# Last round of each stage by token halves, norm intermediates in PSUM, result rows turned by transposes

## The chip, the cores and the metric

The kernel runs on one core of one Trainium2 chip. The metric is the device time of one execution in microseconds (us). Three executions of the kernel before took 2508.81, 2510.29 and 2512.57 us; the median, 2510.29, is the time before.

## What is computed

The program is a backbone of two layers on 1024 latent tokens of width 1024, with 256 context tokens in the first layer. Everything is float32. What matters for the change is this part of the reference:

```python
def swiglu(h, w_gu, w_down):
    gt, up = jnp.split(h @ w_gu, 2, axis=-1)
    return (jax.nn.silu(gt) * up) @ w_down
...
    for l in range(DEPTH):
...
        h = h + g1 * y
        h = h + g2 * swiglu(modulate(rmsnorm(h, norm2_g[l]), sh2, sc2), ffn_w_gu[l], ffn_w_down[l])
...
    return rmsnorm(h, final_g)
```

`y` is the output of a hybrid mixer (attention beside a linear recurrence) in layer 0 and of a short gated convolution in layer 1. `rmsnorm` divides each token by the root of its mean square over the 1024 channels, so a stage can start on a token only when all 1024 channels of the stage before are there. The hidden width of the feed-forward part (FFN) is 2816, which is 11 rounds of 256.

## The kernel before, in words

The stream `h` stays in SBUF, transposed: channels on partitions as 8 tiles of 128, tokens along the free axis. The tokens are worked on as two halves of 512. A product of float32 matrices is made of three matmuls in the reduced type fp32r (`product`, L757 to L759): high part of the weights by high part of the activations, low by high, high by low. A column group (`columns`, L761) is 8 k-steps of these, 24 matmuls of 128x512.

POOL splits each weight tile of 128x1024 into its two parts (`w_hi` L591, `w_lo` L594; for the out projection L690 and L700). SP's queue loads the raw weights some tiles ahead.

The stages on the path are: out projection of the mixer; FFN0 (11 rounds); short convolution mixer (4 rounds); FFN1 (11 rounds); final norm and store. An FFN round is 8 column groups (gate and up of 2 hidden tiles, for token half 0 and then 1; a pair of groups is numbered q = 0 to 3), in which ACT makes silu, DVE the product `hid_f` and ACT and DVE its parts `hid_hi` and `hid_lo`. Then follow 16 down groups (`out_groups`, L792) of 6 matmuls, 8 for token half 0 and 8 for half 1. A short convolution round has 12 column groups and the same 16 down groups. After each down group DVE adds the bank, scaled by the gate, to `h` (`update`, L1434), and two or three banks take turns.

In the last round of a stage the norm of the next stage is woven in. I number these places:

- place 0: out projection to FFN0
- place 1: last round of FFN0 to short convolution
- place 2: last round of the short convolution to FFN1
- the end: last round of FFN1 to the stored result

For each token half, ACT squares the 8 tiles of `h` (`sq`, L1122), DVE adds the squares up in SBUF (`sumsq`: L1388 copies the first, L1391 adds 7), PE sums over partitions (`norm_sum`, L775, four one-column matmuls), ACT takes the root (L1126), DVE the reciprocal and four diagonal matrices (`diag`, L1401, L1403), PE spreads them over the partitions (`norm_spread`, L782). Then for each of 8 tiles DVE makes `scaled` in SBUF (L1410), ACT `act_hi` (L1134), and DVE `act_lo` (L1416). This order of DVE is written out by hand in `last_updates` (L1462): half 1's updates and squares are interleaved with half 0's norm. On PE the sum of half 0 stands behind the 10th down group and its spread behind the 12th; the sum of half 1 stands behind the 16th, ahead of the next stage's first column group, and its spread behind that group:

```python
                    if norm is not None and idx == 9:
                        norm_sum(norm)
                    if norm is not None and norm != N_END and idx == 11:
                        norm_spread(norm)
                if norm is not None and norm != N_END:
                    norm_sum(norm + 1)
```

At the end, `h` is multiplied by a diagonal matrix of the final gains (L1106), which turns it into token rows; DVE (L1801) and ACT (L1373) scale half a row tile each, with two row buffers, and SP stores 512 KB per row tile of 128 tokens.

Of the kernel before, what the change touches and what calls it, by code (L numbers as in the profile page):

```python
# [24 lines left out]
ALU = mybir.AluOpType  # L25
# [33 lines left out]
def backbone(nc, t):  # L59
# [18 lines left out]
    with es:  # L78
# [55 lines left out]
        std = keep("std", [P, 2, 4])  # L134
        x_std = keep("x_std", [P, 3, TT + CT])
# [32 lines left out]
        conv_t = at(84, "conv_t", [P, SEQ])  # L168
# [3 lines left out]
        gain_diag = at(60, "gain_diag", [P, FT, P])  # L172
        fin_rows = at(88, "fin_rows", [P, 2, D])
# [98 lines left out]
        s_tz, s_gdiag = sem("t_pads_zero"), sem("gain_diag_ready")  # L272
        s_fscale, s_fturn, s_store = sem("fin_scale_ready"), sem("fin_turned"), (sem("stored0"), sem("stored1"))
        s_fra, s_frd = sem("fin_row_by_act"), sem("fin_row_by_dve")
# [3 lines left out]
        def alone(eng):  # L278
# [6 lines left out]
                 + [(h, a, HALF, 4, mods, MODS + SH2) for a in (0, 1)]  # L285
                 + [(h, a, HALF, None, None, None) for a in (0, 1)])
        N_X, N_CTX, N_F0, N_S, N_F1, N_END = 0, 2, 3, 5, 7, 9
# [65 lines left out]

        def used_s(i, j):
            return (s_sg, 12 * i + (3, 4, 6, 9, 10, 12)[j]) if j < 6 else (s_out, OUT_S + 16 * i + 16)
# [9 lines left out]
        def _(sp):  # L365
# [195 lines left out]

            for tt in range(TT):
                sp.wait_ge(s_fra, tt + 1)
                sp.wait_ge(s_frd, tt + 1)
                sp.dma_start(out[0, tt * P:(tt + 1) * P, :], fin_rows[:, tt % 2, :]).then_inc(s_store[tt % 2], 16)
            for tt in range(2):
                sp.wait_ge(s_store[tt], 16 * TT // 2)
# [3 lines left out]
        def _(pool):  # L571
# [170 lines left out]
            with pool.Fori(1, FT // 2) as i:  # L742
                for j in range(8):
                    split(8 * i + (U_S + j), j % 4, j % 2, used_s(i - 1, j + 4) if j < 4 else used_s(i, j - 4))
            for j in range(6):
                split(U_F1 + j, j, j % 2, used_s(FT // 2 - 1, j + 4) if j < 4 else used_f(0, ROUNDS - 1, j))
# [6 lines left out]
        def _(pe):  # L753
# [38 lines left out]
            def out_groups(n0, group, norm=None, mod=None):  # L792
# [4 lines left out]
                for idx in range(16):  # L797
# [8 lines left out]
                    if norm is not None and norm != N_END and idx == 11:  # L806
                        norm_spread(norm)
# [1017 lines left out]
```

## Time and profile before

| what | value |
| --- | --- |
| three executions, median | 2510.29 us (2508.81 to 2512.57) |
| the profiled execution | 2510.56 us, its span 2508.4 us |
| PE busy | 2439.4 us, 97% of the span |
| DVE, POOL, ACT busy | 44%, 42%, 21% |
| share of PE in the chain that ended last | 91% |
| granted TensorE clock, mean | 0.988 of full speed |

A row of a timeline gives the start, the time from start to end, the engine, the line and the tiles, and in brackets how long the engine had been idle and what released it. Matmuls overlap: a row lasts some 390 ns, but the next one starts 227 ns later. `x8` beside four instructions means that the profiler records each of these float32 matmuls twice. The granted clock is 1.00 at 2.4 GHz and 0.50 at 1.2 GHz.

### The profile page before, as it was taken

Reading aid. Unit: us, or ns where it says so; the run is one execution under the profiler, and the core shown is the slowest. Engines: PE = TensorE matmul, PEld = TensorE weight load, DVE = VectorE, ACT = ScalarE, POOL = GpSimd, SP = SyncE. Lnnn points to the kernel's source line nnn. Section 1 sums busy time; section 2 is a strip of 40 time slices with the busy share of each in tenths; the row PEclk is TensorE's granted clock in tenths of the full one; section 3 lists DMA queues with packets and bytes.
Section 4 is the critical chain, followed back from the end, with each engine's and each line's share of the span. In section 5 each row is a group of like instructions: output and inputs, shape, how many; then the busy total and the mean of one; then the engine's idle time right before and its main releaser. Section 6 shows DMA issues by size and latency. Waiting matters only on the chain.

```text
span 2508.4 us, 29518 instructions
## 1 busy us (share of the span) xinstructions
PE 2439.4 (97%) x11190; PEld 1994.9 (80%) x11190; DVE 1114.9 (44%) x1433; ACT 528.9 (21%) x811; POOL 1057.6 (42%) x507
## 2 busy tenths in 40 slices
PE   7999999989899999999999899998899999999999
PEld 3788878878788888888887788886788888888887
DVE  5566648856644443422224534346522222222224
ACT  4544428851200000000002200002200000000003
POOL 3233347888533334444443243442543333333340
PEclk9999999999999999999999999999899999999999
DMA  9444465533333333211111011111211111111111
GB/s 302 148 137 150 149 177 95 103 110 101 118 109 100 102 117 117 84 51 50 42 49 43 26 49 44 54 46 34 62 48 47 46 46 46 49 43 50 50 34 68
DMA packets 223197, 206.54 MB, mean 82 GB/s; under 512 B 40119, under 2 KB 193427, under 8 KB 222611
## 3 DMA queue, kind: packets, MB, share of 16 engines
q1 hardware_dynamic: 216643, 186.64, 25.1%
q10 hardware_dynamic: 5904, 16.78, 1.9%
q0 software_dynamic: 576, 2.10, 0.2%
q8 instruction: 51, 0.84, 0.1%
q14 instruction: 23, 0.19, 0.0%
HBM read 185.20 MB, written 20.28 MB: 82 GB/s over the span
## 4 chain that ended last, share of the span: by engine, by line
PE 91%; DVE 4%; issue 2%; ACT 2%; POOL 0%; DMA 0%; ACTq 0%; DVEq 0%; POOLq 0%; SPq 0%
PE bank L757 28%; PE bank L759 28%; PE bank L758 28%; PE bank L893 1%; PE bank L818 1%; DVE probs L1679 1%; PE bank L949 1%; DVE sumsq L1391 1%; PE bank L975 1%; PE bank L974 1%; PE bank L936 1%; PE bank L789 1%; ACT probs L1275 1%; PE bank L937 1%; DVE h L1434 1%
## 5 line engine op out<-in xcount | busy, mean ns | idle before, releaser
L591 POOL TENSOR_TENSOR w_hi<-raw,ones 128x1024 fp32r<-128x1024 f32 x184 | 361.2, 1963 | 1220.0 <-PE bank L759 1164.1
L757 PE MATMUL bank<-act_hi,w_hi 128*128 128x512 f32 x2160 | 846.1, 392 | 3.3 <-DVE act_lo L1555 2.7
L758 PE MATMUL bank<-act_hi,w_lo 128*128 128x512 f32 x2168 | 847.0, 391 | 0.0
L759 PE MATMUL bank<-act_lo,w_hi 128*128 128x512 f32 x2160 | 843.1, 390 | 0.0
L757 PEld LDWEIGHTS bank<-act_hi,w_hi 128*128 128x128 f32 x2160 | 407.5, 189 | 89.7 <-issue 2.8
L758 PEld LDWEIGHTS bank<-act_hi,w_lo 128*128 128x128 f32 x2168 | 409.6, 189 | 84.4
L759 PEld LDWEIGHTS bank<-act_lo,w_hi 128*128 128x128 f32 x2160 | 407.2, 189 | 85.3
L594 POOL TENSOR_TENSOR w_lo<-raw,w_hi 128x1024 fp32r<-128x1024 f32 x184 | 468.0, 2543 | 14.4
L1434 DVE SCALAR_TENSOR_TENSOR h<-bank,mods,h 128x512 f32<-128x512 f32 x432 | 319.7, 748 | 217.2 <-PE bank L759 216.1
L1719 DVE TENSOR_TENSOR hid_f<-silu_g,bank 128x512 f32<-128x512 f32 x88 | 60.5, 688 | 711.2 <-PE bank L759 709.9
L757 PE MATMUL bank<-hid_hi,w_hi 128*128 128x512 f32 x704 | 276.8, 393 | 3.4 <-DVE h L1434 3.2
L759 PE MATMUL bank<-hid_lo,w_hi 128*128 128x512 f32 x704 | 275.1, 391 | 0.0
L758 PE MATMUL bank<-hid_hi,w_lo 128*128 128x512 f32 x704 | 274.5, 390 | 0.0
L757 PEld LDWEIGHTS bank<-hid_hi,w_hi 128*128 128x128 f32 x704 | 132.5, 188 | 34.0 <-DVE h L1434 7.1
L759 PEld LDWEIGHTS bank<-hid_lo,w_hi 128*128 128x128 f32 x704 | 132.4, 188 | 28.5
L758 PEld LDWEIGHTS bank<-hid_hi,w_lo 128*128 128x128 f32 x704 | 132.6, 188 | 27.3
L1338 ACT CAST hid_hi<-hid_f 128x512 fp32r<-128x512 f32 x88 | 54.9, 623 | 449.2 <-DVE hid_f L1719 449.2
L1336 ACT ACT_TABLE_LOAD x20 | 25.7, 1283 | 479.0 <-PE bank L759 478.9
L1336 ACT ACTIVATE silu_g<-bank 128x512 f32<-128x512 f32 x88 | 52.8, 600 | 315.0 <-PE bank L759 314.8
L1722 DVE TENSOR_TENSOR hid_lo<-hid_f,hid_hi 128x512 fp32r<-128x512 f32 x88 | 78.5, 892 | 60.7 <-ACT hid_hi L1338 60.7
L1761 DVE TENSOR_TENSOR t_pad<-cg_sb,bank 128x512 f32<-128x512 f32 x16 | 11.0, 690 | 141.3 <-PE bank L759 141.0
L1275 ACT ACTIVATE probs<-probs,low_all 128x768 f32<-128x768 f32 (+1 forms) x64 | 63.6, 994 | 27.2 <-DVE low_all L1679 26.6
(210 smaller groups left out, 2387.1 us busy)
## 6 DMA issues: line engine op xcount, KB each, us to landing
raw<-in_ffn_w_gu SPq DMA_DIRECT2D x88, 512.0 KB, 3.9
mod_in_f<-in_mod_w SPq DMA_DIRECT2D x48, 512.0 KB, 4.6
raw<-in_ffn_w_down SPq DMA_DIRECT2D x44, 512.0 KB, 3.6
mod_in_p<-in_mod_w SPq DMA_DIRECT2D x32, 512.0 KB, 6.8
raw<-in_o_w_in SPq DMA_DIRECT2D x24, 512.0 KB, 3.7
raw<-in_e_w_in SPq DMA_DIRECT2D x20, 512.0 KB, 5.2
mod_ring<-in_mod_w SPq DMA_DIRECT2D x16, 512.0 KB, 9.5
raw<-in_e_w_out SPq DMA_DIRECT2D x16, 512.0 KB, 3.6
```

The lines of the kernel that those rows point to most:

```text
L591: nc.gpsimd.tensor_tensor(w_hi, raw[:, parity, :], ones[:, 0:1].to_broadcast([P, UNIT]), ALU.mult).then_inc(s_hi, 1)
L594: nc.gpsimd.tensor_tensor(w_lo, raw[:, parity, :], w_hi, ALU.subtract).then_inc(s_split, 1)
L757: pe.matmul(dst, w_hi, x_hi, start=first, stop=False)
L758: pe.matmul(dst, w_lo, x_hi, start=False, stop=False)
L759: return pe.matmul(dst, w_hi, x_lo, start=False, stop=last)
L789: mm = pe.matmul(bank[:, 7, m:m + 1], acc[:, m * P:(m + 1) * P], ones[:, 0:1], start=True, stop=True)
L1275: nc.scalar.activation(probs[s % 3][:, 0:w], probs[s % 3][:, 0:w], ACT.Exp, bias=low_all[:, s:s + 1], scale=-1.0, accum_out=sums[:, s:s + ...
L1336: nc.scalar.activation(silu_g[:, q % 2, :], bank[:, 2 * tile, :], ACT.Silu).then_inc(s_silu, 1)
L1338: nc.scalar.copy(hid_hi[:, tile, half * HALF:(half + 1) * HALF], hid_f[:, q % 2, :]).then_inc(s_hidh, 1)
L1434: V.scalar_tensor_tensor(out=dst, in0=bank[:, from_, :], scalar=mods[:, gate, m:m + 1], in1=dst, op0=ALU.mult, op1=ALU.add).then_inc(s_hup, 1)
L1719: V.tensor_tensor(hid_f[:, q % 2, :], silu_g[:, q % 2, :], bank[:, 2 * tile + 1, :], ALU.mult).then_inc(s_hidf, 1)
L1722: V.tensor_tensor(hid_lo[:, tile, sl], hid_f[:, q % 2, :], hid_hi[:, tile, sl], ALU.subtract).then_inc(s_hid, 1)
```

## The change

The diff runs to some 900 lines. In words:

1. In the last round of FFN0, of the short convolution and of FFN1, all column groups but those of the last tile of half 1 (FFN: q = 3) run first. Then the 8 down groups of half 0, then the groups left out, then the 8 down groups of half 1. The norm of half 0 is done beside q = 3 and the down groups of half 1 (`last_ffn_round`, `last_norms`).
2. The sum over partitions moves into a column group: it stands behind 4 of the 8 k-steps of the group that follows (`first_norm`), and the spread behind that group. This holds for both halves, and for place 0 too, where nothing else of the order changes.
3. `scaled` is written to two PSUM banks (`SCALED`), and the running sum of squares to PSUM bank 7; the last add writes `sumsq` in SBUF, which PE reads. `hid_f` and `z_f` of the part left for later are in a bank too.
4. The first round of the short convolution is ordered so that groups of half 0 come first; the convolution has two buffers.
5. At the end, PE transposes `h` (64 transposes) in place of the products with the diagonal gains. Row tiles 0 to 3 are turned inside q = 3 and the last down groups, and 5 of the 8 parts of row tiles 4 and 5 before the last down group. ACT squares a row tile with its accumulator and takes the root, DVE takes the reciprocal and multiplies 128x1024 by it and by a row of gains. There are four row buffers.

```diff
+        SCALED = {3: 2, 4: 4, 5: 0, 6: 4, 7: 2, 8: 4}
...
             def scale(n, f):
                 src, half, w, gain, *_ = NORMS[n]
                 dve.wait_ge(s_bc, n + 1)
-                dve.wait_ge(s_norm, 8 * n + f - 2)
-                V.scalar_tensor_tensor(out=scaled[:, (8 * n + f) % 3, 0:w], in0=src[:, f, cols(n)], scalar=gains[:, gain, f:f + 1],
+                dve.wait_ge(s_norm, 8 * n + f - 1)
+                V.scalar_tensor_tensor(out=bank[:, SCALED[n] + f % 2, 0:w], in0=src[:, f, cols(n)], scalar=gains[:, gain, f:f + 1],
                                        in1=bank[:, SPREAD[n], 0:w], op0=ALU.mult, op1=ALU.mult).then_inc(s_scal, 1)
...
-                    V.tensor_tensor(sumsq[:, 0:w], sumsq[:, 0:w], sq[:, f % 2, 0:w], ALU.add).then_inc(s_sum, 1)
+                    if f == FT - 1 and n > N_F0:
+                        dve.wait_ge(s_ss, n - N_F0)
+                    to = sumsq[:, 0:w] if f == FT - 1 else bank[:, 7, 0:w]
+                    V.tensor_tensor(to, bank[:, 7, 0:w], sq[:, f % 2, 0:w], ALU.add).then_inc(s_sum, 1)
```

New functions of PE (`gate_up` is one pair of groups, `half_down` 8 down groups; the fourth argument of `last_ffn_round` is None for FFN1):

```python
            def first_norm(n):
                return ({4: lambda: norm_sum(n)}, None), lambda: norm_spread(n)
...
                for q in range(3):
                    gate_up(layer, i, u0, norm_in, q)
                half_down(0, (2, 3))
                pe.wait_ge(s_hup, n0 + 6)
                if norm_out is not None:
                    gate_up(layer, i, u0, norm_in, 3, *first_norm(norm_out))
                    half_down(1, ())
                else:
                    gate_up(layer, i, u0, norm_in, 3, ({3: lambda: fin_early(0)}, {2: lambda: fin_early(1), 6: lambda: fin_early(2)}))
                    half_down(1, (), {4: lambda: fin_early(3), 6: lambda: fin_late((4, 5), range(4)), 7: lambda: fin_late((4, 5), (4,))})
```

New on DVE (`mid` holds the product of q = 3, at the third tile), and the row at the end:

```python
                def between(f):
                    if f in mid:
                        mid[f]()
                    if 3 <= f < 7:
                        for m in (2 * f - 6, 2 * f - 5):
                            update(n0, FT + m, gate, 4 + m % 2)

                apply_norm(n, between)
                for f in range(FT):
                    add_squares(n + 1, f)
                inverse_rms(n + 1)
                apply_norm(n + 1)
...
                V.reciprocal(fin_scale[:, tt:tt + 1], fin_rms[:, tt:tt + 1]).then_inc(s_fscale, 1)
...
                V.scalar_tensor_tensor(out=fin_rows[tt % 4][:], in0=bank_f[:, b * HALF:(b + 2) * HALF], scalar=fin_scale[:, tt:tt + 1],
                                       in1=gain_row[:], op0=ALU.mult, op1=ALU.mult).then_inc(s_fin, 1)
```

The order on DVE at place 1, while the norm of half 0 is applied. Before, each tile of the norm goes with an update and an add of half 1's squares:

```order
L1410 SCALAR_TENSOR_TENSOR scaled<-h,gains,bank 128x512 x2
L1416 SCALAR_TENSOR_TENSOR act_lo<-scaled,mods,act_hi 128x512
L1410 SCALAR_TENSOR_TENSOR scaled<-h,gains,bank 128x512
L1434 SCALAR_TENSOR_TENSOR h<-bank,mods,h 128x512
L1391 TENSOR_TENSOR sumsq<-sumsq,sq 128x512
L1416 SCALAR_TENSOR_TENSOR act_lo<-scaled,mods,act_hi 128x512
```

Now:

```order
L1630 SCALAR_TENSOR_TENSOR bank<-h,gains,bank 128x512
L1968 TENSOR_TENSOR bank<-silu_g,bank 128x512
L1971 TENSOR_TENSOR hid_lo<-bank,hid_hi 128x512
L1636 SCALAR_TENSOR_TENSOR act_lo<-bank,mods,act_hi 128x512
L1630 SCALAR_TENSOR_TENSOR bank<-h,gains,bank 128x512
L1653 SCALAR_TENSOR_TENSOR h<-bank,mods,h 128x512 x2
L1636 SCALAR_TENSOR_TENSOR act_lo<-bank,mods,act_hi 128x512
```

and behind the last tile of that norm:

```order
L1636 SCALAR_TENSOR_TENSOR act_lo<-bank,mods,act_hi 128x512
L1608 COPY bank<-sq 128x512
L1614 TENSOR_TENSOR bank<-bank,sq 128x512 x6
L1614 TENSOR_TENSOR sumsq<-bank,sq 128x512
L1621 RECIPROCAL std<-std 128x4
```

The product of q = 3 moved in, the updates come in pairs, and all eight squares of half 1 are added up behind the norm of half 0.

The order on PE at place 1, from the last down group into the short convolution. Before:

```order
L759 MATMUL bank<-hid_lo,w_hi 128x512
L775 MATMUL bank<-ones,sumsq 128x1 x4
L757 MATMUL bank<-act_hi,w_hi 128x512
L758 MATMUL bank<-act_hi,w_lo 128x512
L759 MATMUL bank<-act_lo,w_hi 128x512
```

Now the sum stands behind 12 matmuls of the first group, of which the last three are:

```order
L788 MATMUL bank<-act_hi,w_hi 128x512
L789 MATMUL bank<-act_hi,w_lo 128x512
L790 MATMUL bank<-act_lo,w_hi 128x512
L808 MATMUL bank<-ones,sumsq 128x1 x4
L788 MATMUL bank<-act_hi,w_hi 128x512
```

The sum moved 12 matmuls back; those need only half 0, whose norm is done.

The order on PE at the very end (`ident` is the identity, `h` the stream; L878 is the transpose). It is now:

```order
L790 MATMUL bank<-hid_lo,w_hi 128x512
L878 MATMUL bank<-ident,h 128x128 x2
L788 MATMUL bank<-hid_hi,w_hi 128x512
L789 MATMUL bank<-hid_hi,w_lo 128x512
L790 MATMUL bank<-hid_lo,w_hi 128x512
L788 MATMUL bank<-hid_hi,w_hi 128x512
L789 MATMUL bank<-hid_hi,w_lo 128x512
L790 MATMUL bank<-hid_lo,w_hi 128x512
L878 MATMUL bank<-ident,h 128x128 x22
```

22 of the 64 transposes stand behind the last down group; the other 42 moved ahead of it.

## Rows read from the trace of the kernel before

**Rows 1.** Window over the four up and gate stretches of a round: busy us, clock, DMA.
```profile
1309.25:1352.78 43.53, 43.53 (x193) 36.05 (x192) 5.31 (x7) 4.28 (x7) 21.73 (x10) 1.00 0.17 49
```

**Rows 2.** Timeline of PE, place 0: start, us, instruction, idle before in brackets.
```profile
597.08 0.95 PE L775 MATMUL bank<-ones,sumsq 128*128 128x1 f32 x8
...
639.79 1.86 PE L775 MATMUL bank<-ones,sumsq 128*128 128x1 f32 x8 [7.69 <-DVE sumsq L1391]
...
688.08 0.39 PE L757 MATMUL bank<-hid_hi,w_hi 128*128 128x512 f32 x1
```

**Rows 3.** Timeline of PE, place 1, FFN0 to short convolution.
```profile
1352.78 0.39 PE L757 MATMUL bank<-hid_hi,w_hi 128*128 128x512 f32 x1
...
1375.72 0.50 PE L757 MATMUL bank<-hid_hi,w_hi 128*128 128x512 f32 x1 [2.31 <-DVE h L1434]
...
1388.56 1.87 PE L775 MATMUL bank<-ones,sumsq 128*128 128x1 f32 x8 [6.03 <-DVE sumsq L1391]
1390.29 0.77 PE L757 MATMUL bank<-act_hi,w_hi 128*128 128x512 f32 x1
...
1397.26 1.05 PE L782 MATMUL bank<-diag,ones 128*128 128x128 f32 x8
1398.07 0.48 PE L757 MATMUL bank<-act_hi,w_hi 128*128 128x512 f32 x1
...
1459.28 0.40 PE L757 MATMUL bank<-z_hi,w_hi 128*128 128x512 f32 x1
```

**Rows 4.** Timeline of PE, place 2, short convolution to FFN1.
```profile
1721.24 0.40 PE L757 MATMUL bank<-z_hi,w_hi 128*128 128x512 f32 x1
...
1763.81 1.86 PE L775 MATMUL bank<-ones,sumsq 128*128 128x1 f32 x8 [12.73 <-DVE sumsq L1391]
...
1811.59 0.39 PE L757 MATMUL bank<-hid_hi,w_hi 128*128 128x512 f32 x1
```

**Rows 5.** Timelines of DVE and of POOL, place 2.
```profile
1749.86 0.76 DVE L1416 SCALAR_TENSOR_TENSOR act_lo<-scaled,mods,act_hi 128x512 fp32r<-128x512 f32 x1
...
1753.59 2.82 DVE L1416 SCALAR_TENSOR_TENSOR act_lo<-scaled,mods,act_hi 128x512 fp32r<-128x512 f32 x1
1756.34 0.73 DVE L1410 SCALAR_TENSOR_TENSOR scaled<-h,gains,bank 128x512 f32<-128x512 f32 x1
1756.99 0.74 DVE L1434 SCALAR_TENSOR_TENSOR h<-bank,mods,h 128x512 f32<-128x512 f32 x1
...
1768.93 2.80 DVE L1403 TENSOR_SCALAR diag<-ident,std 128x128 f32<-128x128 f32 x4
...
1753.20 2.67 POOL L594 TENSOR_TENSOR w_lo<-raw,w_hi 128x1024 fp32r<-128x1024 f32 x1
```

**Rows 6.** Windows of 2 us at place 1; the number behind the busy times is the granted clock.
```profile
1376.00:1378.00 2.00, 2.00 (x6) 1.19 (x5) 2.00 (x4) 0.94 (x2) 0.00 (x0) 0.56 0.00 0
1390.00:1392.00 2.00, 2.00 (x7) 1.71 (x7) 1.05 (x5) 0.27 (x1) 0.00 (x0) 0.50 0.00 0
```

**Rows 7.** Timeline of DVE, place 2, where POOL runs nothing.
```profile
1738.98 0.42 DVE L1388 COPY sumsq<-sq 128x512 f32<-128x512 f32 x1
1739.50 0.69 DVE L1391 TENSOR_TENSOR sumsq<-sumsq,sq 128x512 f32<-128x512 f32 x1
```

**Rows 8.** Timelines at the end: the last down matmul and the last half row.
```profile
2488.09 0.39 PE L759 MATMUL bank<-hid_lo,w_hi 128*128 128x512 f32 x1
...
2504.51 0.75 DVE L1801 TENSOR_SCALAR fin_rows<-bank,fin_scale 128x512 f32<-128x512 f32 x1 [0.75 <-DMA out<-fin_rows]
```

**Rows 9.** Timeline of PE in the attention stage, and the window around it.
```profile
442.26 0.82 PE L949 MATMUL bank<-ident,probs 128*128 128x128 f32 x6
442.84 0.48 PE L974 MATMUL bank<-pt_hi,v_odd 128*128 128x512 f32 x1
...
442.00:444.00 2.00, 2.00 (x14) 1.79 (x13) 1.41 (x4) 1.75 (x4) 1.92 (x2) 1.00 1.05 257
```

**Rows 10.** Group of ACT by line and shape: busy us, mean ns, idle before by releaser.
```profile
L1122 ACT ACTIVATE sq<-h 128x512 f32<-128x512 f32 x64 | 40.0, 632 | 93.6 <-DVE h L1434 92.1 <-DVE sumsq L1388 1.4
```

More of the change, by code:

```diff
@@ L1014, in _, with gate_up @@
             out_groups(0, out_group, N_F0)
-            def ffn_round(layer, i, u0, norm_in, norm_out=None, mod=None, first=False):
+            def gate_up(layer, i, u0, norm_in, q, at_k=None, then=None):
+                q0 = 4 * ROUNDS * layer
+                half, tile = divmod(q, 2)
+                pe.wait_ge(s_hidf, 4 * i + (q0 + q + 1))
+                for a in range(2):
+                    if half == 0:
+                        pe.wait_ge(s_split, 6 * i + (u0 + 2 * tile + a + 1))
+                    columns(bank[:, 2 * tile + a, :], 2 * tile + a, act_hi, act_lo,
+                            slice(half * HALF, (half + 1) * HALF), norm_in + half,
+                            at_k[a] if at_k is not None else None).then_inc(s_gu, 1)
+                    if then is not None and a == 0:
+                        then()
@@ new lines, in short_tile @@
+            def short_tile(i, tile, banks=(0, 2), halves=range(2)):
+                for half in range(2):
+                    cg_copy(i, tile, half, banks[half])
+                for half in halves:
+                    z_high(i, tile, half)
+            short_tile(0, 0, (2, 1))
+            short_tile(0, 1, (1, 0))
+            with act.Fori(1, SHORT_LAST) as i:
+                for tile in range(2):
+                    short_tile(i, tile)
+            short_tile(SHORT_LAST, 0, (0, 2), (0,))
@@ new lines, in short_tile @@
+            def short_tile(i, tile, banks=(1, 3), gates_=(0, 1)):
+                for half in range(2):
+                    short_half(i, tile, half, banks)
+                short_conv(i, tile)
+                for half, b in enumerate(gates_):
+                    short_z(i, tile, half, b)
+            short_tile(0, 0, (3, 2), (0, 3))
+            short_tile(0, 1, (2, 3), (1, 2))
+            for idx in range(16):
+                update(OUT_S, idx, MODS + G1, 4 + idx % 3)
+            with dve.Fori(1, SHORT_LAST) as i:
+                steps.begin_loop(i - 1, 6)
+                for tile in range(2):
+                    short_tile(i, tile)
+                for idx in range(16):
+                    update(16 * i + OUT_S, idx, MODS + G1, 4 + idx % 3)
```

537 lines of the change are left out of this document (351 added, 186 removed).

## The prediction

> **What bounds the kernel now.** I read first the chain of waits: it is TensorE's matmuls for 91% of the span, so only what stops TensorE costs time. Then a window over one stretch of column groups: 192 matmuls in 43.53 us at a granted clock of 1.00, which is 0.2267 us each, with PE busy all the time [rows 1]. Nothing can be won there. Then the timeline of PE for its idle brackets. They stand at the places where a norm lies between two stages. I take each place from its first to its last row, and subtract 0.2267 us for each matmul and 0.81 us for each of the four small blocks (two sums, two spreads); 0.81 is the step from 1397.26 to 1398.07 [rows 3].
>
> - Place 0: 688.08 - 597.08 = 91.00; 336 matmuls are 76.17, blocks 3.24; **11.6 us too much**, 7.69 of it the wait ahead of half 1's sum [rows 2].
> - Place 1: 106.50; 384 matmuls are 87.05, blocks 3.24; **16.2 us too much**: waits of 2.31 and 6.03 and what follows them [rows 3].
> - Place 2: 90.35; 288 matmuls are 65.29, blocks 3.24; **21.8 us too much**, the sum's wait alone 12.73 [rows 4].
> - The end: from the last down matmul at 2488.09 to 2508.40 it takes **20.3 us** [rows 8].
>
> What DVE does in the waits shows two causes. It has a long list between the two norms. And an operation with both tensors in SBUF is slowed while POOL splits weights: act_lo takes 0.76 us alone and 2.82 with POOL's w_lo beside it, while scaled and h, which read a bank, keep 0.73 and 0.74 at the same time [rows 5]. A third cost follows: after a wait TensorE runs slower. At place 1 the granted clock is 0.56 after the first wait and 0.50 after the second [rows 6], that is near the lower level of 1.2 GHz. Behind the second wait the sum took 1.73 us (not 0.81) and the first 24 matmuls 6.97 (not 5.44) [rows 3]: **2.45 us per such wait**.
>
> **Prices.** A DVE operation with one bank operand starts 0.65 us after the one before (1756.34 to 1756.99, rows 5); I use 0.66. No row shows one with a bank both read and written, which scaled, the copy and the adds now are. The surcharge of one bank operand can be bounded: the add of two SBUF tiles lasts 0.69, an update 0.74 [rows 5, 7]. So from 0 to 0.12 us more than now (an estimate: twice that difference). I take 0.73 for each of the eight square operations, since each waits for the one before (0.69 and a handover), and 0.66 for the rest. A rule speaks against the copy: it took 0.42 from SBUF to SBUF [rows 7]. The Trainium skill, "VectorE: DVE Perf Modes", section "Why PSUM operands drop a tier", says that a PSUM operand keeps fp32 out of the faster modes; no run here shows it yet. By the row the copy would stay at 0.42 and each place be 0.3 us shorter; by the rule it is as I have it.
>
> **Place 0.** The order on DVE stays, only tiles move to PSUM, and the sum moves behind 12 matmuls. DVE now has some 25 operations of 0.66 to 0.73, 17.5 us, ahead of the sum, from 610 on: done long before the last down matmul at 631.72 (639.79 less 7.69 less 0.39). What is late next is the last update's chain: 0.39 + 0.10 to the bank, update 0.74, square 0.63 [rows 10], add 0.69, with handovers: ready at 634.4. TensorE gets there at 631.72 + 0.23 + 12 x 0.2267 = 634.67. No wait, and no fall of the clock. The diagonals stay in SBUF and may still take 2.80 [rows 5] where 2.72 of matmuls and the block cover them: 0.7 left. Of the 11.6, some 0.9 belongs to neither wait nor clock, and I leave as much again for DVE's lag: 2.5 stay, **9.1 gained**.
>
> **Place 1.** Between half 0's spread and half 1's sum, DVE does 16 norm operations and 8 updates (24 x 0.66 = 15.84), 8 on squares (8 x 0.73 = 5.84), and for q = 3 hid_f, a cast by ACT and hid_lo (2.1, as DVE waits for ACT): 23.8. I add 2.1 for waits for ACT's first square, its halves and its reloads of tables (an estimate): 25.9. TensorE has in that time the second group (24), 48 down matmuls and 12 of the next group, 84 x 0.2267 = 19.04. So **6.9 us of wait stay**, and with them 2.45 for the clock. The hidden parts are late for the first down group of half 1, and updates for its banks: 0.95. Together 10.3 of 16.2: **5.9 gained**. POOL runs nothing there, so this is the order alone.
>
> **Place 2.** Two tiles' z for half 1 take the place of one hidden tile: 2.1 more, 28.0; less 19.04 leaves 9.0. Then 2.45 for the clock; a wait of 2.0 for the z of half 1, by the length of ACT's and DVE's steps on it, with a fall of the clock that costs 2.1 (the wait of 2.31 at place 1 had one, rows 3, 6); small ones 1.0. Together 16.5 of 21.8: **5.3 gained**. That POOL no longer slows act_lo is in this, since all of DVE's list now has at most one SBUF input but the diagonals.
>
> **The end.** Ahead of the last matmul come 42 transposes. Six took 0.58 (442.26 to 442.84, rows 9), 0.10 each; a row of a float32 block gives 0.81/4 = 0.20 each. I take 0.125, 5.25 together (bounds 4.1 and 8.5). The hidden parts of q = 3 are late by 1.0, turns of banks 0.5, while the sum and its block fall away (0.8): the last matmul is **6.0 later**. Behind it: matmul and handover 0.49, update 0.74, the last transposes 0.45, then ACT's squares and roots row tile by row tile: 1.1 each for 4 and 5, 2.2 each for 6 and 7 (two squares of 0.63 [rows 10] and small operations), DVE's last 128x1024 with its reciprocal 1.5 (two times 0.66 and a little), the store as now, 2508.40 - 2505.26 = 3.14 [rows 8], and 0.6 of handovers: 13.5. **20.3 - 13.5 = 6.8 won, 6.0 lost: 0.8 gained.** The reordered first round of the short convolution I cost at nothing: TensorE has no wait there, and DVE's work is hidden behind 24 matmuls per group; without that cover it would be a few tenths.
>
> **Sum.** 9.1 + 5.9 + 5.3 + 0.8 = 21.1. From the profiled execution, 2510.56: 2489.5. The median is 0.27 lower: **2489.2 us**.
>
> **Rivals.**
> - *A, DVE stays the bound by more.* Bank to bank costs 0.12 more in 16 operations (1.9) and the waits for ACT are 4 instead of 2: at places 1 and 2 3.9 us more each, at place 0 a short wait comes back with its clock, 4. Together 11.8: **2501**. For it: DVE's list is longer than TensorE's cover at places 1 and 2 in my own count. Against: ACT was never late there before.
> - *B, slower: the clock at the end.* 42 transposes stand among the last 96 matmuls. If TensorE's clock fell to its lower level over q = 3 and the last down groups, 96 x 0.2267 + 5.3 = 27 us would become 54: 2489.2 + 27 = **2516**. It decides against the change from 21 us at half clock on. Against it: with six transposes in two microseconds the attention stage has a granted clock of 1.00 [rows 9], and TensorE is never idle beside these. The Trainium skill, "TensorE: Matmul & The Clock Gate", Part 4 ("PE-mode transpose"), says that a transpose "doesn't count as PE-busy the same way"; by that rule the clock would be at risk, and the attention row does not bear it out.
> - *C, the tiles in PSUM do not do what they should.* If POOL slowed DVE whatever its operands, the order alone would help: place 0 keeps 7.69 less the 2.72 of the 12 matmuls and its clock, so gains some 3, place 2 about 1, places 1 and the end as above: 10.7, **2499.6**. Against it: scaled and h beside act_lo [rows 5]. The Trainium skill, "SBUF — State Buffer", section "Who interferes with whom", has it that only a second SBUF input contends, which would exclude C; the trace agrees for operations that read a bank, none shows one that also writes it.
> - *D, no change*: transposes at 0.20 (3.2 more), A and a longer tail: 2506 to 2510.
>
> **Chances.** Forecast 0.66, A 0.18, C 0.07, D 0.04, B 0.04, and 0.01 for the rest. The range goes down to **2480**, where the clock does not fall at places 1 and 2 (7.0) and bank operands cost nothing more and 2 more are won from waits; it goes up to **2501**, taking in A and C. Forecast's own range is 2482 to 2496. No difference that a measurement can tell is within 0.2%, 5 us: faster means below 2505.3. From the cases: forecast, A (but its upper end) and C make 0.91 faster; D 0.04 within; B and the rest 0.05 slower.
>
> **What would show it.** Right: PE's wait for sumsq under 1 us at place 0, with the granted clock at 1.00; 4 to 9 us of such waits at places 1 and 2, followed by a clock near 0.50; scaled, act_lo and adds below 0.8 us beside POOL; the last matmul near 2473 in the trace, and 13 to 14 us behind it. Wrong: waits for sumsq gone at places 1 and 2 (I overcounted DVE); act_lo above 2 us (C); a granted clock under 0.9 after 2440 (B).

## The result and the profile after

The changed kernel takes 2494.11 us in the median (2492.61 to 2495.64), the kernel before 2510.28. The ratio is 0.9935 with a 95% interval of 0.9922 to 0.9947: **16.2 us or 0.65% faster**. The forecast was 2489.2, range 2480 to 2501. Sign and range held; the gain was three quarters of the 21.1 us of the sum, and its parts were off in both directions.

The page of the changed kernel, busy times, granted clock and chain:

```profile
PE 2427.5 (97%) x11110; PEld 1983.5 (80%) x11110; DVE 1078.7 (43%) x1415; ACT 529.3 (21%) x825; POOL 1053.0 (42%) x507
...
PEclk9999999999999999999999999999999999999999
...
PE 92%; DVE 4%; ACT 2%; issue 1%; POOL 0%; ACTq 0%; DVEq 0%; POOLq 0%
```

PE is busy 12 us less than before (2439.4), with the same large matmuls and fewer small ones; the other 6 us of the gain are idle time. To see where, I cut the timeline of PE into the same stretches in both kernels. Place 1 runs here from the first matmul of FFN0's last round, place 2 from that of the last short convolution round, each up to the first down matmul of the next round; the end from the last FFN1 round's first matmul.

| stretch, us | before | after | gained | forecast |
| --- | --- | --- | --- | --- |
| start to the first sum of place 0 | 597.08 | 595.03 | 2.05 | 0 |
| place 0 | 91.00 | 86.19 | 4.8 | 9.1 |
| place 1 | 150.03 | 146.60 | 3.4 | 5.9 |
| short convolution, rounds 0 to 2 | 196.63 | 197.80 | -1.2 | 0 |
| place 2 | 155.68 | 149.95 | 5.7 | 5.3 |
| the end | 87.05 | 84.13 | 2.9 | 0.8 |
| all FFN rounds between | 1230.97 | 1231.10 | -0.1 | 0 |

The 2.05 us ahead of place 0 are no work of the change: in the profiles of the fourteen kernels of this study, whose first part is the same, the first sum starts anywhere from 593.83 to 597.08 us. Without it the profiled runs differ by 15.6 us, which fits the medians.

**Place 0.** PE's timeline in the changed kernel, and behind it DVE's, POOL's and two windows. A window gives its start, end and length, then the busy us and the number of instructions of PE, PE's weight loads, DVE, ACT and POOL, then the granted clock, the share of the DMA engines and GB/s:

```profile
633.18 1.05 PE L808 MATMUL bank<-ones,sumsq 128*128 128x1 f32 x8 [0.83 <-DVE sumsq L1614]
...
640.52 2.08 PE L815 MATMUL bank<-diag,ones 128*128 128x128 f32 x8 [3.43 <-DVE diag L1623]
642.25 0.77 PE L788 MATMUL bank<-act_hi,w_hi 128*128 128x512 f32 x1
...
630.94 0.74 DVE L1636 SCALAR_TENSOR_TENSOR act_lo<-bank,mods,act_hi 128x512 fp32r<-128x512 f32 x1
...
634.79 5.68 DVE L1623 TENSOR_SCALAR diag<-ident,std 128x128 f32<-128x128 f32 x4
...
634.07 1.90 POOL L618 TENSOR_TENSOR w_hi<-raw,ones 128x1024 fp32r<-128x1024 f32 x1
...
638.00:640.00 2.00, 0.00 (x0) 0.00 (x0) 2.00 (x2) 0.00 (x0) 2.00 (x2) 1.00 0.03 9
642.00:644.00 2.00, 2.00 (x7) 1.69 (x7) 1.36 (x2) 0.58 (x1) 0.85 (x1) 0.52 1.01 360
```

The sum's wait went from 7.69 us [rows 2] to 0.83, and act_lo takes 0.74 us beside POOL (2.82 before, rows 5). But now the spread waits 3.43 us for the diagonals. These four 128x128 operations, 0.88 us alone and 2.80 in [rows 5], took 5.68 us, and the clock fell behind the wait to 0.52. One by one they took 1.26, 0.28, 2.44 and 1.93 us: three of them ended within 0.1 us of the end of a POOL operation. A wait took the place of the one removed.

**Places 1 and 2.** The waits of PE, and DVE's list at place 1:

```profile
1362.74 0.50 PE L788 MATMUL bank<-hid_hi,w_hi 128*128 128x512 f32 x1 [1.36 <-DVE hid_lo L1971]
...
1381.69 1.87 PE L808 MATMUL bank<-ones,sumsq 128*128 128x1 f32 x8 [4.95 <-DVE sumsq L1614]
...
1732.31 0.50 PE L788 MATMUL bank<-z_hi,w_hi 128*128 128x512 f32 x1 [3.14 <-DVE z_lo L2031]
...
1752.03 1.86 PE L808 MATMUL bank<-ones,sumsq 128*128 128x1 f32 x8 [4.95 <-DVE sumsq L1614]
...
1357.63 0.75 DVE L1636 SCALAR_TENSOR_TENSOR act_lo<-bank,mods,act_hi 128x512 fp32r<-128x512 f32 x1
1358.48 0.76 DVE L1630 SCALAR_TENSOR_TENSOR bank<-h,gains,bank 128x512 f32<-128x512 f32 x1
...
1376.13 4.72 DVE L1614 TENSOR_TENSOR bank<-bank,sq 128x512 f32<-128x512 f32 x6
1380.94 0.69 DVE L1614 TENSOR_TENSOR sumsq<-bank,sq 128x512 f32<-128x512 f32 x1
...
1376.92 0.63 ACT L1279 ACTIVATE sq<-h 128x512 f32<-128x512 f32 x1 [0.17 <-DVE bank L1614]
...
1384.00:1386.00 2.00, 2.00 (x6) 1.61 (x5) 0.94 (x5) 0.00 (x0) 0.00 (x0) 0.50 0.00 0
```

Both sums are 4.95 us late, where they were 6.03 and 12.73 [rows 3, 4]. The clock still falls behind them: 0.50, and the 12 matmuls behind the sum at place 1 take 4.97 us in place of 2.72. From an act_lo to the next scaled DVE now steps 0.85 us, not 0.66. The six adds take 4.72 us, 0.79 each: each waits for ACT's square, and that for a buffer of an add. At place 2, PE also waits 3.14 us for the z of half 1.

The 3.4 us that place 1 gained can be split by counting what PE spends over 0.2267 us a matmul. The 96 down matmuls cost 6.4 us over before and 4.1 now, 2.3 gained; the sum's wait gave 0.9. The matmuls between the sum and the spread, slowed by the clock in both, cost 0.7 more. Behind the last spread 1.36 us over became 0.11, which is 1.25 gained by the reordered first short convolution round: before, three matmuls were held up there by act_lo of half 1 (the longest recorded wait is 0.36).

**The end.** The last down matmul, the last row, and a window in which PE transposes between matmuls:

```profile
2478.20 0.39 PE L790 MATMUL bank<-hid_lo,w_hi 128*128 128x512 f32 x1
...
2486.41 1.28 DVE L1740 SCALAR_TENSOR_TENSOR fin_rows<-bank,fin_scale,gain_row 128x1024 f32<-128x1024 f32 x1
...
2450.00:2460.00 10.00, 10.00 (x53) 8.41 (x52) 2.20 (x3) 5.48 (x7) 0.00 (x0) 1.00 0.13 53
```

From the last matmul to 2490.80 it takes 12.60 us (20.3 before, rows 8), and the stretch ahead of that matmul is 4.83 us longer. The granted clock is 1.00 with 16 transposes among the matmuls of that window.

### The profile page after: what moved, and what is told of

It reads as the page before. It is cut to its first block, busy times and chain, and to the rows that moved or that the text cites. A ratio compares the mean times of both kernels' runs of the same rounds, so it can differ in the third digit from the quotient of the medians.

```text
span 2490.8 us, 29258 instructions
## 1 busy us (share of the span) xinstructions
PE 2427.5 (97%) x11110; PEld 1983.5 (80%) x11110; DVE 1078.7 (43%) x1415; ACT 529.3 (21%) x825; POOL 1053.0 (42%) x507
## 3 DMA queue, kind: packets, MB, share of 16 engines
HBM read 185.73 MB, written 20.28 MB: 83 GB/s over the span
## 4 chain that ended last, share of the span: by engine, by line
PE 92%; DVE 4%; ACT 2%; issue 1%; POOL 0%; ACTq 0%; DVEq 0%; POOLq 0%
PE bank L788 28%; PE bank L790 28%; PE bank L789 28%; PE bank L976 1%; PE bank L901 1%; DVE probs L1928 1%; PE bank L1032 1%; PE bank L1058 1%; PE bank L1057 1%; PE bank L1019 1%; PE bank L822 1%; ACT probs L1477 1%; PE bank L1020 1%; DVE bank L1614 0%; DVE h L1653 0%
```

## The experiments

Edits are shown in part; `...` marks what is left out. before_psum, before_sum_inside, before_both and tiles_sbuf take the change apart, with two theories. **Theory 1**, mine: where POOL runs, DVE is slowed in operations with both tensors in SBUF; the rest is DVE's list against TensorE's cover. **Theory 2**: the order is what counts. Where theory 2 says something else, the expectation tells. All stretches are taken as above, each from the one profiled execution of its kernel. The time before is the median of all its executions beside these runs (2510.2 to 2510.4 each time).

| kernel | median | place 0 | place 1 | short | place 2 | the end |
| --- | --- | --- | --- | --- | --- | --- |
| before | 2510.4 | 91.0 | 150.0 | 196.6 | 155.7 | 87.0 |
| changed | 2494.1 | 86.2 | 146.6 | 197.8 | 150.0 | 84.1 |
| before_psum | 2504.5 | 86.8 | 153.6 | 196.6 | 151.3 | 87.3 |
| before_sum_inside | 2506.2 | 89.8 | 148.3 | 196.6 | 157.3 | 87.1 |
| before_both | 2500.2 | 87.3 | 150.3 | 196.6 | 149.9 | 87.3 |
| before_two_buffers | 2514.4 | 91.0 | 153.4 | 196.6 | 157.6 | 87.0 |
| tiles_sbuf | 2506.9 | 91.6 | 150.8 | 197.8 | 154.2 | 84.2 |
| end_late | 2502.4 | 86.1 | 146.6 | 197.8 | 150.0 | 93.1 |
| end_late_banks | 2498.1 | 86.2 | 147.2 | 197.8 | 150.5 | 87.0 |
| diag_act | 2488.8 | 80.9 | 146.5 | 197.8 | 151.5 | 84.2 |
| sum_later | 2489.8 | 87.0 | 144.1 | 197.8 | 148.0 | 84.1 |
| squares_early | 2474.4 | 81.2 | 138.8 | 197.8 | 144.0 | 84.2 |
| z_early | 2474.6 | 81.2 | 138.9 | 197.8 | 143.0 | 84.2 |
| scale_last | 2474.1 | 81.8 | 138.8 | 197.8 | 142.2 | 84.2 |

A stretch moves by up to 1.5 us with how long the clock stays down behind the same waits: diag_act has at place 2 the waits of the changed kernel (3.16 and 4.95 us, there 3.14 and 4.95) and takes 1.5 us more, all of it in the matmuls behind the second wait and in the spread. Differences of about a microsecond between two rows of a place are not told apart by this table.

### before_psum: the tiles in PSUM alone

```diff
-                dve.wait_ge(s_norm, 8 * n + f - 2)
+                dve.wait_ge(s_norm, 8 * n + f - 1)
...
-                V.scalar_tensor_tensor(out=scaled[:, (8 * n + f) % 3, 0:w], in0=src[:, f, cols(n)], scalar=gains[:, gain, f:f + 1],
+                V.scalar_tensor_tensor(out=bank[:, SCALED[n] + f % 2, 0:w], in0=src[:, f, cols(n)], scalar=gains[:, gain, f:f + 1],
...
-                    V.tensor_tensor(sumsq[:, 0:w], sumsq[:, 0:w], sq[:, f % 2, 0:w], ALU.add).then_inc(s_sum, 1)
+                    to = sumsq[:, 0:w] if f == FT - 1 else bank[:, 7, 0:w]
+                    V.tensor_tensor(to, bank[:, 7, 0:w], sq[:, f % 2, 0:w], ALU.add).then_inc(s_sum, 1)
```

> The kernel before, with scaled and the running sum of squares in PSUM; its order untouched. Theory 1 (beside POOL, DVE is slowed where both tensors of an operation lie in SBUF): act_lo and the adds stay at 0.7 to 0.8 us beside POOL; the sum's wait falls from 7.69 to about 2.5 us at place 0 and from 12.73 to about 6 at place 2, place 1 stays within 0.5 us; the diagonals, still in SBUF, take over 2.8 us at place 0. Time 12 to 14 us under the kernel before, about 2497. Theory 2 (the order is what counts): the waits stay within 2 us of before, time 2507 to 2510.

Measured: ratio 0.9972 (0.9960 to 0.9983). DVE at place 0, and PE's waits at places 0 and 2:

```profile
632.38 0.74 DVE L1418 SCALAR_TENSOR_TENSOR act_lo<-bank,mods,act_hi 128x512 fp32r<-128x512 f32 x1
...
636.86 4.99 DVE L1405 TENSOR_SCALAR diag<-ident,std 128x128 f32<-128x128 f32 x4
...
634.63 1.68 PE L776 MATMUL bank<-ones,sumsq 128*128 128x1 f32 x8 [3.55 <-DVE sumsq L1393]
...
1756.98 1.86 PE L776 MATMUL bank<-ones,sumsq 128*128 128x1 f32 x8 [5.56 <-DVE sumsq L1393]
```

act_lo is fast beside POOL, and the waits fell about as theory 1 had it (3.55 us at place 0 where it said 2.5, 5.56 at place 2 where it said 6; the diagonals took 4.99). With the kernel's order untouched, this shows both the contention and its cure. But place 1, where both theories saw nothing, lost 3.6 us, and the total was 7 us short of what theory 1 gave.

### before_two_buffers: why place 1 lost

```diff
-                dve.wait_ge(s_norm, 8 * n + f - 2)
-                V.scalar_tensor_tensor(out=scaled[:, (8 * n + f) % 3, 0:w], in0=src[:, f, cols(n)], scalar=gains[:, gain, f:f + 1],
+                dve.wait_ge(s_norm, 8 * n + f - 1)
+                V.scalar_tensor_tensor(out=scaled[:, f % 2, 0:w], in0=src[:, f, cols(n)], scalar=gains[:, gain, f:f + 1],
```

> The kernel before, with two buffers for scaled in SBUF in place of three, so that each scaled waits for the act_lo just ahead of it. Theory 1 (the pair of PSUM banks costs 0.19 us a tile through this wait, not through PSUM): DVE's step from act_lo to the next scaled grows from 0.66 to 0.85 us at place 1, and place 1 takes 2.5 to 4 us more, as it did with the tiles in PSUM (153.6 in place of 150.0). Theory 2 (writing PSUM is what is dear): place 1 stays within 0.5 us of 150.0.

Measured: ratio 1.0015 (1.0005 to 1.0024), place 1 at 153.4, beside 153.6 with the tiles in PSUM. DVE at place 1:

```profile
1377.84 0.75 DVE L1416 SCALAR_TENSOR_TENSOR act_lo<-scaled,mods,act_hi 128x512 fp32r<-128x512 f32 x1
1378.69 0.75 DVE L1410 SCALAR_TENSOR_TENSOR scaled<-h,gains,bank 128x512 f32<-128x512 f32 x1
```

The step is 0.85 us, in SBUF as in PSUM. Theory 1 holds: a bank costs DVE nothing that shows (0.74 to 0.76 us for each of these operations). What costs is a turn of two: scaled of tile f + 2 must wait for the end of act_lo of tile f, just ahead of it on the same engine. That is 0.19 us for each of six tiles, 1.1 us, ahead of the sum and again behind its spread; the remaining 1.0 of the 3.3 us lost is the clock, behind a sum's wait of 6.60 in place of 6.03.

### before_sum_inside: the sum inside a group alone

```diff
                 for k in range(FT):
+                    if k == 4 and at_k is not None:
+                        norm_sum(at_k)
...
-                if norm is not None and norm != N_END:
-                    norm_sum(norm + 1)
```

> The kernel before, with the sum of half 1 moved behind 12 matmuls of the next stage's first group, the spread still behind that group; all tiles stay in SBUF. Theory 1: the sum's waits fall by 2.7 us at each place, but at places 0 and 2 the diagonals (2.8 us, behind two act_lo of 5.1 us, both slowed by POOL) are then late for the spread, and a wait of some 3.5 us ahead of it takes the gain back; only place 1 gains, 2.7 us, or 5 if the clock does not fall. Time 2505 to 2508. Theory 2: 2.7 us and the clock's 2.45 at each place, 2495 to 2500.

Measured: ratio 0.9980 (0.9971 to 0.9990). At place 2, DVE and the wait behind it:

```profile
1756.37 5.13 DVE L1418 SCALAR_TENSOR_TENSOR act_lo<-scaled,mods,act_hi 128x512 fp32r<-128x512 f32 x2
1761.42 0.16 DVE L1403 RECIPROCAL std<-std 128x4 f32<-128x4 f32 x1
1761.62 6.52 DVE L1405 TENSOR_SCALAR diag<-ident,std 128x128 f32<-128x128 f32 x4
...
1768.20 2.08 PE L784 MATMUL bank<-diag,ones 128*128 128x128 f32 x8 [5.24 <-DVE diag L1405]
```

The time is theory 1's, its parts only in kind. The sum's waits fell by 2.72 and 2.74 us at places 0 and 1 (7.69 to 4.97, 6.03 to 3.29), as said. At place 2 it fell by 7.31 (12.73 to 5.42), in part since one act_lo and one add fewer met POOL's splits ahead of the sum; and there the spread then waited 5.24 us behind two act_lo in 5.13 and four diagonals in 6.52. At place 0 it waited 1.01, not 3.5. Place 1 gained 1.7 where 2.7 was expected, place 0 1.2, and place 2 lost 1.7. The sum's step by itself is worth little.

### before_both: the two together

> Both edits together on the kernel before: tiles in PSUM and the sum inside the first group; no halves order, and the old end. Theory 1: place 0 as in the changed kernel (about 5 us gained), place 1 some 3 to 5 gained, place 2 some 9 to 11 gained: about 2491 to 2493, so the order by halves of the last round adds nothing at places 1 and 2. Theory 2 (the order by halves brings its own gain there): 2 to 5 us more than the changed kernel at places 1 and 2 together, 2498 to 2503.

Measured: ratio 0.9957 (0.9940 to 0.9974), 10.2 us under before. The time fits theory 2, the places show why. Place 0 is as in the changed kernel but for 1.1 us, with nearly the same wait for the diagonals (3.34); the 1.1 us are slower matmuls behind the spread (2.0 us over 0.2267 each, 0.9 in the changed kernel), so the clock. Place 2 gained 5.8, as much as the changed kernel and not the 9 to 11 I expected. Place 1 gained nothing (150.3), as the turn of two ate what the sum won. So **the order by halves and the reordered first short round are worth 3.7 us at place 1 and nothing at place 2**, and the changed kernel gives 1.2 of it back in the short convolution rounds. By PE's timeline the 3.7 are 2.6 in the down groups and 2.35 behind the spread, the part of the short round, less 1.1 of a longer wait for the sum. No run has the one without the other.

### tiles_sbuf: the changed kernel without scaled in PSUM

```diff
-                V.scalar_tensor_tensor(out=bank[:, SCALED[n] + f % 2, 0:w], in0=src[:, f, cols(n)], scalar=gains[:, gain, f:f + 1],
+                V.scalar_tensor_tensor(out=scaled[:, f % 2, 0:w], in0=src[:, f, cols(n)], scalar=gains[:, gain, f:f + 1],
```

> The changed kernel, with scaled back in SBUF (two buffers), all else as changed; the sums stay in PSUM. Theory 1: act_lo takes 2.5 to 2.9 us where POOL runs: place 0 loses 4 to 6 us, place 1 some 2 to 3 (POOL splits four tiles there beside the norm of half 0), place 2 some 6 to 8: about 2508. Theory 2 (where the tile lies does not matter in this order): within 2 us of the changed kernel, 2492 to 2496.

Measured: ratio to before 0.9986 (0.9977 to 0.9996), 12.8 us over the changed kernel: place 0 lost 5.4, places 1 and 2 4.2 each. DVE at place 0, one act_lo and then the last two with the diagonals:

```profile
632.09 1.28 DVE L1636 SCALAR_TENSOR_TENSOR act_lo<-scaled,mods,act_hi 128x512 fp32r<-128x512 f32 x1
...
634.74 3.69 DVE L1636 SCALAR_TENSOR_TENSOR act_lo<-scaled,mods,act_hi 128x512 fp32r<-128x512 f32 x2
...
638.56 6.53 DVE L1623 TENSOR_SCALAR diag<-ident,std 128x128 f32<-128x128 f32 x4
```

Theory 1 holds, with the total at 2506.9 for 2508; of its parts place 1 lost more than the 2 to 3 us said and place 2 less than the 6 to 8. Where scaled lies carries most of the gain of the changed kernel: four fifths of 16.2 us go with it. That is against two buffers in SBUF; with three, as the kernel before has, it may be less, and I did not run that. In this order the spread at place 0 waits 5.68 us.

### diag_act: the diagonals by ACT

```diff
+                for j in range(NORMS[n][2] // P):
+                    last = nc.scalar.activation(diag[:, j, :], ident[:], ACT.Copy, scale=std[:, 1, j:j + 1])
+                last.then_inc(s_rstd, 1)
...
-                for j in range(w):
-                    last = V.tensor_scalar(diag[:, j, :], ident[:], std[:, 1, j:j + 1], None, ALU.mult)
-                last.then_inc(s_rstd, 1)
```

> The changed kernel, with the four diagonal matrices of each norm written by ACT (a copy scaled per partition) in place of DVE. Theory 1 (at place 0 the gain is held back by the diagonals alone, two SBUF tensors on DVE beside POOL, 5.68 us): ACT takes about 1.0 us for the four, the 3.43 us wait ahead of the spread and the clock's fall behind it go, place 0 falls from 86.2 to about 81 us, the other places stay within 0.3; 5 us under the changed kernel, 2489. Theory 2 (place 0 is held by something else, such as act_hi's latency or the loads, and the diagonals only stand last): place 0 keeps over 84 us, 2492 to 2494.

Measured: 2488.79 us (2488.60 to 2490.87), ratio to before 0.9914 (0.9897 to 0.9930), 5.3 under the changed kernel. ACT and PE at place 0:

```profile
636.75 1.28 ACT L1288 ACTIVATE diag<-ident,std 128x128 f32<-128x128 f32 x4 [0.24 <-DVE std L1626]
...
638.90 1.05 PE L816 MATMUL bank<-diag,ones 128*128 128x128 f32 x8
```

The four take 1.28 us beside POOL's split, the spread has no wait, and place 0 falls from 86.2 to 80.9: theory 1, to 0.1 us. Everything I missed at place 0 was in the diagonals; the wait of 0.83 us at the sum is still there. Place 2 was to stay within 0.3 us and took 1.5 more in this profile. Its waits did not change, the clock behind them did: in the last 2 us ahead of the spread it is 0.50 here and 0.82 in the changed kernel (second row).

```profile
1753.64:1755.64 2.00, 2.00 (x6) 1.52 (x5) 0.00 (x0) 0.00 (x0) 0.00 (x0) 0.50 0.00 0
...
1755.92:1757.92 2.00, 2.00 (x8) 1.57 (x8) 0.00 (x0) 0.00 (x0) 0.00 (x0) 0.82 0.29 86
```

### sum_later: more cover ahead of the sum

```diff
-                short_group(0, 0, 0, 0, 2, (s_hid, 4 * ROUNDS), sums[0])
-                spread()
-                short_group(0, 0, 1, 0, 3, (s_zf, 2))
+                short_group(0, 0, 0, 0, 2, (s_hid, 4 * ROUNDS))
+                norm_sum(N_S + 1)
+                short_group(0, 0, 1, 0, 3, (s_zf, 2), {4: lambda: norm_spread(N_S + 1)})
```

> The changed kernel, with the sum of half 1 behind the whole first group of the next stage (24 matmuls in place of 12) and the spread behind 12 matmuls of the second group, at all three places. Theory 1 (places 1 and 2 are short of cover for DVE's list): the waits of 4.95 fall to 2.2 and the clock stays up, each place gains 2.7 for the wait and 2.5 for the clock; place 0 gains 0.8: 2483 to 2486. Theory 2 (the late norm then holds the groups of half 1 or the banks that hid_f must free): the wait moves there, gain 0 to 3 us, 2491 to 2494.

Measured: 2489.83 us (2489.23 to 2491.05), ratio 0.9920 (0.9903 to 0.9936). PE at place 1 and the clock behind its wait:

```profile
1382.92 1.87 PE L808 MATMUL bank<-ones,sumsq 128*128 128x1 f32 x8 [2.23 <-DVE sumsq L1613]
...
1384.00:1386.00 2.00, 2.00 (x7) 1.79 (x8) 0.84 (x5) 0.26 (x1) 0.00 (x0) 0.50 0.00 0
```

The wait fell to 2.23 us as said, and place 1 gained 2.5, place 2 2.0, so the wait's part came. The clock's part did not: behind 2.23 us the granted clock is again 0.50. At place 2, whose wait was 2.23 us too, it fell again. Place 0 lost 0.8: its wait only moved to the diagonals (3.92). Both theories had part of it wrong: the waits did not move to other groups, and the clock did not stay up.

### squares_early: both, and three adds moved up

```diff
-                        for m in (2 * f - 6, 2 * f - 5):
-                            update(n0, FT + m, gate, 4 + m % 2)
+                        update(n0, FT + 2 * f - 6, gate, 4)
+                        if f in (4, 6):
+                            add_squares(n + 1, f // 2 - 2 + f // 6)
+                        update(n0, FT + 2 * f - 5, gate, 5)
+                        if f == 5:
+                            add_squares(n + 1, 1)
...
-                for f in range(FT):
+                for f in range(3, FT):
                     add_squares(n + 1, f)
```

> Both edits (diagonals by ACT, sum later), and on DVE three of the eight adds of half 1's squares moved up between the updates, where DVE waits for banks. Theory 1: DVE's list behind the last update is some 1.5 us shorter, the sum's waits at places 1 and 2 under 1 us; 2481 to 2484. Theory 2 (the updates come later by the adds, and TensorE waits for the banks of the down groups instead): no better than the two edits alone, 2484 to 2488.

Measured: **2474.44 us (2473.91 to 2475.44), ratio to before 0.9858 (0.9842 to 0.9875)**, 19.7 under the changed kernel. At place 1:

```profile
1374.22 0.39 PE L791 MATMUL bank<-act_lo,w_hi 128*128 128x512 f32 x1
1374.57 1.05 PE L809 MATMUL bank<-ones,sumsq 128*128 128x1 f32 x8
...
1374.00:1376.00 2.00, 2.00 (x13) 1.57 (x12) 0.56 (x2) 1.22 (x2) 0.00 (x0) 1.00 0.00 0
1376.00:1378.00 2.00, 2.00 (x10) 1.64 (x9) 0.13 (x1) 1.28 (x4) 0.00 (x0) 1.00 0.00 0
```

Theory 1's direction, and 7 us more than it gave. The sum has no wait any more, and the clock stays at 1.00 through it: the sum takes 0.91 us, the 12 matmuls behind it 2.83, where sum_later had 1.73 and 5.19. Place 1 is 5.2 us under sum_later for a wait of 2.23: the rest is the clock, 3.2 (0.82 in the sum, 2.36 behind it), less 0.2 of a longer wait for a bank. At this place the clock cost as much behind 2.23 us as behind 4.95. At place 2 the same step gave 4.0. If sum_later's 4.3 us and diag_act's 5.3 simply added up, the time would be 2484.5; the measured time is 10 us below that. How much of the 10 the three adds make by themselves is not shown: the two edits without the adds, and the adds without them, were not run.

### end_late and end_late_banks: no rows beside the last round

```diff
-                    gate_up(layer, i, u0, norm_in, 3, ({3: lambda: fin_early(0)}, {2: lambda: fin_early(1), 6: lambda: fin_early(2)}))
-                    half_down(1, (), {4: lambda: fin_early(3), 6: lambda: fin_late((4, 5), range(4)), 7: lambda: fin_late((4, 5), (4,))})
+                    gate_up(layer, i, u0, norm_in, 3)
+                    half_down(1, ())
```

> The changed kernel, with all 64 transposes behind the last down group, none beside the last round; squares, roots and rows as changed. Theory 1 (the early half is worth its price by little): the last down matmul comes 4.5 us earlier, the stretch behind it grows from 12.6 to some 17.5 to 18.5 us, as ACT needs 1.5 us for each of eight row tiles: 0.5 to 1.5 us slower, 2495. Theory 2 (doing rows beside the last round is where the end's gain comes from): 4 us or more slower, 2498 and above.

Measured: 2502.39 us (2500.17 to 2504.91). The end took 93.1 us, 9 more than in the changed kernel, as theory 2 said (4 or more). But PE's transposes waited for rows of DVE that held the same banks, 4.33, 1.34 and 0.72 us, and the run could not tell the place of the transposes from the turn of banks. So the second run, with four pairs of banks in turn:

```diff
-        FIN_BANK = (6, 6, 0, 6, 2, 0, 6, 4)
+        FIN_BANK = (6, 0, 2, 4, 6, 0, 2, 4)
```

> As end_late, but row tiles take four pairs of banks in turn (6, 0, 2, 4), so that three transposed row tiles never wait for one pair. Theory 1: the 4.3 + 1.3 + 0.7 us that transposes waited for rows in end_late go, the stretch behind the last matmul is 18 to 20 us, ACT's 1.5 us for a row tile its bound; 2496 to 2498, so rows beside the last round are worth 2 to 3 us. Theory 2 (the banks were not it): 24 us or more, 2501 or above.

Measured: 2498.09 us (2497.06 to 2498.64); behind the last matmul 20.28 us, the whole end 87.0, as the kernel before had (87.05). So rows beside the last round are worth 2.9 us, all that the end gained, and the new way of making rows nothing by itself.

### z_early and scale_last: two more steps at place 2

```diff
-                       {0: lambda: short_z(SHORT_LAST, 0, 1, 0), 2: lambda: short_z(SHORT_LAST, 1, 1, 1)})
+                       {0: lambda: short_z(SHORT_LAST, 0, 1, 0), 1: lambda: short_z(SHORT_LAST, 1, 1, 1)})
```

> As squares_early, with the second z of half 1 in the last short round made behind the second tile of the norm, not behind the third. Theory 1 (the wait of 3.14 us at place 2 is DVE's order): it falls by 1.5 us, place 2 from 144.0 to 142.5; 2473. Theory 2 (it is the latency from DVE to ACT and back): within 0.3 us, 2474.5.

Measured: 2474.61 us (2472.69 to 2475.04), not to be told from squares_early. In the profile the wait for z fell from 3.14 to 1.65 us, as theory 1 had it, but a wait of 2.03 us for an update came behind it; place 2 gained 1.0. The waits of its down groups are 0.4 us longer in sum; the gain is the clock, which stayed at 1.00 behind both of them, where it had been 0.50 behind the 3.14. The window behind the 2.03:

```profile
1721.00:1723.00 2.00, 1.62 (x7) 1.36 (x8) 1.90 (x4) 0.99 (x2) 2.00 (x1) 1.00 0.66 193
```

```diff
                     low(n, f)
+                    between(f)
                     if f + 2 < FT:
                         scale(n, f + 2)
-                    between(f)
```

> As z_early, with scaled of tile f+2 behind the updates and adds that stand between two tiles, so that its wait for act_lo is covered by them. Theory 1 (0.19 us a tile is a wait for a buffer): DVE's list is 0.8 us shorter beside half 1's updates, the waits for banks of the down groups shorter by as much; 0 to 1.5 us faster than z_early. Theory 2: act_hi now comes later, and act_lo waits for ACT: 0 to 2 us slower.

Measured: 2474.13 us (2473.57 to 2474.53), ratio 0.9854 (0.9838 to 0.9871), within the spread of the two before it. Place 2 gained 0.9, place 0 lost 0.6 to a wait for act_lo, place 1 did not move. Neither theory is told from the other by a time so small.

## Why the prediction was right or wrong

**Right.** The sign, the range, and the main mechanism: DVE's SBUF operations beside POOL. act_lo fell from 2.82 to 0.74 us, and undoing only that costs 12.8 us. That the total came within 5 us is in part luck: place 0 fell 4.3 us short and place 1 2.5, the end gave 2.1 more, and place 2 came out right by two errors against each other. Of the signs named, the last matmul near 2473 did not come; it stands at 2478.20. Rival C is out. Rival A's price for a bank is out (0.69 to 0.76 us an operation), though a wait with its clock did come back at place 0, for another cause. Rival B is out too: with transposes between the matmuls of the last round the granted clock is 1.00, and the Trainium skill's remark in "TensorE: Matmul & The Clock Gate", Part 4, that a transpose does not count as busy in the same way, made no difference to the clock here, where matmuls stood around them.

**Place 0, 9.1 forecast, 4.8 measured.** The step that failed is "the diagonals ... may still take 2.80 where 2.72 of matmuls and the block cover them: 0.7 left". The price came from a row in which only the first of the four, 2.21 us, ran into a POOL operation and the other three took 0.28 each. They took 5.68 us, the wait was 3.43, and the clock cost 1.7 more (0.92 in the spread, 0.8 behind it); diag_act returned 5.3. The Trainium skill, "SBUF — State Buffer", section "Who interferes with whom", says that a DVE operation in a two-port mode and a GpSimd one lock each other out for a whole instruction, whoever issues first, and names tensor_scalar among those that can. By that rule each of four short operations can wait out a long one. The trace agrees: the four took 1.26, 0.28, 2.44 and 1.93 us, beside w_hi of 1.90, w_lo of 2.48 and the next w_hi of 1.89. The same section of the Trainium skill has it that ACT never waits on another engine, and here ACT took 1.28 for the four. Rival C quotes the section as if only a second SBUF input contended; that leaves out the two-port modes, the case of the diagonals.

**Place 1, 5.9 forecast, 3.4 measured.** "6.9 us of wait stay" was 4.95; what failed is 0.95 for the hidden parts and banks, and 2.45 for the clock. The two runs of 48 down matmuls took 11.89 and 13.97 us, 4.1 over 21.76, of which 2.8 are waits for updates and for hid_lo (0.69, then 1.36, 0.51 and 0.21); and the clock cost 3.2 (1.72 for the sum, 4.97 for 12 matmuls). The first short round, "cost at nothing", gave 1.25. That DVE's step from act_lo to scaled is 0.85 us and not 0.66 with two buffers was nowhere in my prices: I bounded what PSUM may cost, and the cost was in the wait that came with it. The bound on PSUM itself held, at its lower end.

**Place 2, 5.3 forecast, 5.7 measured**: right as a sum, and that is luck. The wait for z was 3.14 and not 2.0, the sum's 4.95 and not 9.0. The sum's wait and its clock came out 3.9 us under their two terms (11.45), and the down groups 3.1 over theirs (5.1 with the wait for z and its clock, where 8.2 were spent, among them a wait of 1.23 us for z in half 0's down groups that I had not seen). My list for DVE counted all eight adds at 0.73 behind 28 us of work; in truth DVE waits for banks in between, and the list's tail behind the last update (act_lo, a copy, seven adds: 1374.68 to 1381.63, 6.95 us, against 2.72 of matmuls) is what makes the wait, the same 4.95 at both places.

**The end, 0.8 forecast, 2.9 measured**: the last matmul was 4.8 later, not 6.0, as eight transposes took 0.79 us, 0.10 each and not 0.125; the stretch behind it was 12.6, not 13.5.

**Not foreseen and not settled**: each group of six down matmuls in short convolution rounds 0 to 2 takes 1.400 us, not 1.374, 1.2 us in all. Every kernel built on the changed one has it, none built on the one before; no row shows a wait, and I tried nothing on it.

## What to carry to other kernels

When one operation is cured of a contention, price every operation that stays exposed in the same minute, and by its worst overlap, not by one row. When a tile moves to a scarcer memory, count the buffers: a turn of two puts the consumer's end into the producer's start. And when a wait of TensorE is being shortened, look at what the clock does behind it: here the last 2.23 us of two waits were worth 5.2 and 4.0, since the clock's fall went with them. So a few operations moved to an idle engine or into an idle moment (diagonals to ACT, three adds, the sum one group later) brought more than the whole change.

## What the hardware showed that I had not expected

- Four 128x128 tensor_scalar operations of DVE, 0.88 us alone, took 2.80 to 6.53 us beside POOL's 128x1024 operations; the same four on ACT took 1.28.
- A wait of 2.23 us ahead of a sum (sum_later, place 1) had a granted clock of 0.50 behind it. Behind 0.83 us at place 0, 1.36 at place 1, and 1.65 and 2.03 at place 2 of z_early it stayed at 1.00. Length alone does not decide: a wait of 2.31 us in the down groups of place 1 had 0.56 behind it in the kernel before [rows 6] and 1.00 in before_sum_inside (1375 to 1377).
- DVE's operations with a bank as an input, an output or both take as long here as those in SBUF: scaled 0.75 to 0.76, act_lo 0.74, add 0.69. The copy went from 0.42 to 0.68 or 0.69, as the Trainium skill's "Why PSUM operands drop a tier" in "VectorE: DVE Perf Modes" had it.
